# Decay gates moved into the input projection, the last down projection made a branch of the expert loop, and wide products beside the router

## The chip, the cores and the metric

The kernel runs on one core of a Trainium2 chip. The metric is the device time of one execution in microseconds (us). A core has a matrix engine (TensorE, PE, which reads its weights in a separate step, PEld), two elementwise engines (VectorE, DVE, and ScalarE, ACT), a third one (GpSimd, POOL) that here mostly issues gathers and scatters, and SyncE (SP), which issues the other transfers. Each has an instruction queue of its own and runs it in order; they wait for one another on semaphores.

## The reference

One encoder layer over 1024 tokens of width 1024, in float32:

```python
h = rms_norm(x)
q, k, v, r, gf, gb, glu = split(h @ w_in)          # gf, gb: 16 columns each
la_f = log_sigmoid(gf @ w2_f + b_f) / 16           # decay per token and key column
la_b = log_sigmoid(gb @ w2_b + b_b) / 16
a = rms_norm(gla(q,k,v,la_f) + flip(gla(flipped,la_b))) * silu(r)   # 4 heads, dk 64, dv 128
b = silu(layer_norm(depthwise_conv31(glu_a * sigmoid(glu_g))))
x = x + concat(a, b) @ w_out
x = x + cross_attention(rms_norm(x), rms_norm(mem))                 # 256 memory tokens, 4 heads
h = rms_norm(x)
gates = softmax(top4(h @ router_w + router_b))     # 32 experts
x = x + sum over the 4 experts of gate * (swiglu(h @ w_up + b_up) @ w_down + b_down)
y = rms_norm(x)
```

The decays `la` are summed up along the tokens inside windows of 128; scores and states use exponentials of differences of these sums, so the sums of a head pair must exist before any scores but those of the first level can be made.

## The kernel before

**Order of the stages.** The order of work is written out by hand for each engine, in one block an engine. PE's block runs: transposes of the normed x; input projection; LayerNorm sums of the convolution branch; memory projections mixed with the gated linear attention (GLA) of head pair 0; pair 1; output projection; queries, cross attention and its output projection; router; expert visits; last down projection. Times in the profile for these: projection from 36 to 275 us, GLA up to 527, output projection to 621, cross attention to 930, router to 971, expert visits from 1029 to 2578, last down projection from 2598.6, final norm from 2634.6.

**Input projection.** `w_in` comes in eleven chunks of 256 columns over a ring of buffers (SP's loop over `chunks`; a load waits for the matmul group named in `used`). ACT rounds each chunk to fp32r (`wiH`, line 670), DVE makes the rest (`wiL`, L1240, `w_in_lo`), and PE multiplies three products of high and low parts per 128 rows (L1946). Groups are numbered by `n` over eight PSUM banks: a group with n of 8 or more waits for the drain of group n-7. Groups 0 and 1 are the 32 gate columns; ACT copies them to `gT` (L699). Chunks 1 to 4 are the two GLU halves, drained by ACT to `u_pad` (L706) and by a sigmoid (L716), and DVE starts the 31-tap convolution (L1295, L1299, 124 steps) after `w_in_lo(4)`. Group 18 and the following are queries and keys, then values and `r`.

**Gates.** After the LayerNorm of the convolution branch, `gates(p)` (PE, L2032) multiplies `gT` by the second gate matrix for the head pair p, four matmuls into banks 0 to 3. ACT takes the absolute value from PSUM (L792), then Exp (L795) and Ln (L797) in place in `KQ`. DVE takes the minimum with 0 (L1345, into `EX`), subtracts (L1352), sums each window by a scan (L1356, into `Bf` and `Rb`, 16 scans), copies the window totals to `TTd` (L1362, L1363) and turns the second direction into suffix sums (L1365, L1367). For pair 0 this stands ahead of its scores; for pair 1, `gates(1)` comes after pair 0's keys are turned, the minima come before pair 0's states (L1429), and the rest after the multiplication of `r` by the norm's gain (L1459), before the exponents of pair 1 (L1383). `Bf` and `Rb` are shared by both pairs. Pair 0's scores use `exponents`, an exponential on ACT (L806), products on DVE (L1402, L1404) and small matmuls (L2057), level by level; `memory_chunk` (L1985) lies between them on PE and is drained by ACT (L663). PE waits at `gates(0)` for the end of LayerNorm.

**Router.** For each of eight token tiles PE turns the tile by eight transposes (L2255) and then multiplies the tile before by the router's weights, eight matmuls of 32 columns (L2245, 16 records). DVE makes top-4 and positions from it.

**Experts.** There are `last_` + 1 visits, here 32 (`last_` is a register read from memory, here 31). A visit's weights come in chunks of 1 MB (`load_chunk`), ACT rounds them (`split_hi`, L1014) and DVE makes the low part (`lo_by_vector`, L1740). Each engine has a loop `Fori(1, NVIS)` with NVIS = 53 and, inside, one `If(t <= last_)`; the passes with t above `last_` (21 of them) do nothing but count and test. What is left of the last visit, its second half of down-projection weights (chunks 15 to 18) and the matmuls, drains and scatter on them, stands after the loop. Then SP reloads the sums, ACT squares them (L1168), DVE scales them (L1901 to L1909), and SP stores them.

**Base rows.** Before the loop SP loads chunks 4 to 7 of visit 0, stores the residual rows to `acc_dram` tile by tile as they become ready (`s_bdr`), waits for all eight, and goes on with chunks 8 and 9.

Of the kernel before, what the change touches and what calls it, by code (L numbers as in the profile page):

```python
# [59 lines left out]
EARLY_BASE = 6  # L60
# [5 lines left out]
def build(nc, A):  # L66

    with ExitStack() as ctx:
# [77 lines left out]
        TTd = sb("TTd", [P, 2, 2, TT], F, 203.25)  # L146
# [92 lines left out]
        for n in ("m", "x", "y", "z"):  # L239
# [12 lines left out]
        s_z, s_zabs, s_zln, s_zmin, s_la, s_scan, s_tot, s_rb, s_dec = (  # L252
            sem(n) for n in ("gate_product", "gate_abs", "gate_softplus", "gate_min", "log_decay", "scanned",
# [57 lines left out]
        used = ([("in", n) for n in (2, 6, 10, 14, 18, 22, 26, 34, 42, 54, 62)]  # L311
# [85 lines left out]
        def _(sp):  # L397
# [10 lines left out]

            for i in range(4):
                sp.dma_start(xres[:, 2 * i:2 * i + 2, :], x_in[:, 2 * i:2 * i + 2, :]).then_inc(s_xld[i], 16)  # L410
            for g, (w, c0) in enumerate(chunks):
                if 2 <= g < N_IN + NR:
                    last = used[min(g, N_IN + 1) - 2]
                    sp.wait_ge(s_mm[last[0]], last[1])
                elif g >= NR:
                    sp.wait_ge(s_mm[used[g - NR][0]], used[g - NR][1])
                if g == g_out:
                    sp.wait_ge(s_ket, 8)
                if g == g_out + 1:
                    sp.wait_ge(s_op, 32)  # L420
                sp.dma_start(ring[:, slot_of[g]], w[:, c0:c0 + 256].rearrange("(k p) n -> p k n", p=P)
                             ).then_inc(s_ring[slot_of[g]], 16)
                if g == 1:
# [40 lines left out]
            for t in range(TT):  # L464
                sp.wait_ge(s_bdr, 2 * (t + 1))
                sp.dma_start(acc_dram[P * t:P * (t + 1), :], xres[:, t, :]).then_inc(s_acc, 16)
            sp.wait_ge(s_acc, 16 * TT)
            for c in range(8, 4 + NRAW):
                load_chunk(0, c, e0, None, fresh=True)
            for c in range(4 + NRAW, 12):  # L470
# [3 lines left out]
            with sp.Fori(1, NVIS) as t:  # L474
# [6 lines left out]
            e_last = expert(last_)  # L481
            for c in range(15, 19):
                load_chunk(last_, c, None, e_last, last=True)
# [13 lines left out]
        def _(pool):  # L497
# [105 lines left out]
            with pool.Fori(1, NVIS) as t:  # L603
# [5 lines left out]
            scatter(last_)  # L609
# [3 lines left out]
        def _(act):  # L613
# [81 lines left out]
            for th in range(2):  # L695
# [5 lines left out]
                next_split()  # L701
            for c2 in range(2):
# [17 lines left out]
            for dst, sc in ((qT, GDK ** -0.5), (kT, 1.0)):  # L720
                for ft in range(2):
                    for th in range(2):
                        d = drain("in", n)
                        if n == 18:
                            act.wait_ge(norms["x"]["scaled"], TT)
# [26 lines left out]
            for c in range(CT):  # L752
                act.wait_ge(s_lnv, 2 * (c + 1))
                if c == 0:
                    act.wait_ge(s_mm["in"], 62)
# [30 lines left out]
            def softplus(p):  # L786
                if p:
                    act.wait_ge(s_gram, 16)
                for n in range(4):
                    d, th = n // 2, n % 2  # L790
                    act.wait_ge(s_z, 4 * p + n + 1)
                    nc.scalar.activation(KQ[:, d, 512 * th:512 * (th + 1)], PS[:, n, :], ACT.Abs,  # L792
                                         bias=PV[:, ZB + 2 * d + p:ZB + 2 * d + p + 1]).then_inc(s_zabs, 1)
                act.wait_ge(s_zabs, 4 * (p + 1))
                nc.scalar.activation(KQ[:], KQ[:], ACT.Exp, scale=-1.0).then_inc(s_zln, 1)  # L795
                act.wait_ge(s_zln, 2 * p + 1)
                nc.scalar.activation(KQ[:], KQ[:], ACT.Ln, bias=1.0).then_inc(s_zln, 1)  # L797

            def window_decays(p):
                act.wait_ge(s_tot, 2 * (p + 1))  # L800
                nc.scalar.activation(TTd[:, 1], TTd[:, 0], ACT.Exp, scale=1.0 / TAU).then_inc(s_dec, 1)
# [51 lines left out]
            softplus(0)  # L853
# [20 lines left out]
            softplus(1)  # L874
# [259 lines left out]
            with act.Fori(1, NVIS) as t:  # L1134
# [16 lines left out]
            both_last = has_tail(last_)  # L1151
            split_hi(last_, 15)
            for c in range(16, 19):
                wait_lo(act, last_, c - NSPL)
                split_hi(last_, c, first=True)
            drain_rows(last_ + 1, 0, both_last, c0=1)
# [1290 lines left out]
```

## Time and profile before

| | us |
|---|---|
| median of 3 runs | 2657.73 (2645.79 to 2658.1) |
| the profiled execution | 2655.09 |
| its span | 2653.3 |
| PE busy | 2399.1 (90%) |
| DVE busy | 1814.8 (68%) |
| ACT busy | 1286.2 (48%) |
| POOL busy | 366.5 (14%) |
| DMA | 523.03 MB, mean 197 GB/s |

A row of a timeline gives the start from the span's beginning, the length, engine, line, operation, tensors and shapes, the number of instructions in the row, and in brackets the idle time before it with what ended it; "issue" there is a wait for nothing that the profile shows. PE's matmuls are pipelined, so a row's length is a little more than the spacing of its instructions. PEclk is the granted clock of PE as a share of the full one. An fp32 matmul shows as two records, an fp32r one as one.

### The profile page before, as it was taken

How to read it: one execution, taken by the hardware profiler on the slowest of the kernel's cores; microseconds unless marked ns; L12 is line 12 of the kernel's file. 1: busy time of each engine (PE TensorE's matmuls, PEld its weight loads, DVE VectorE, ACT ScalarE, POOL GpSimd, SP SyncE). 2: the span in 40 equal slices, each digit the busy share in tenths (PEclk: the TensorE clock that was granted, in tenths of full speed). 3: DMA queues.
4: the chain of work that ended last, by engine and by line, in shares of the span. 5: the costliest groups of instructions: out<-in, count | busy, mean ns of one | idle time of the engine just before them, and what ended most of it. 6: DMA issues, size and time to landing. Idle time of an engine off the chain costs nothing.

```text
span 2653.3 us, 38454 instructions
## 1 busy us (share of the span) xinstructions
PE 2399.1 (90%) x13540; PEld 1952.5 (74%) x13605; DVE 1814.8 (68%) x1880; ACT 1286.2 (48%) x1418; POOL 366.5 (14%) x305
## 2 busy tenths in 40 slices
PE   6999785698978977899999999999999999999983
PEld 5889574497846975777777777787787777777762
DVE  4499588614043157788977787778777778988763
ACT  4212455403132124656755565566555556766543
POOL 0000000010000042122211211122122112222210
PEclk9999896698999959899999999999999999999996
DMA  3111210311100028989987897789787789999764
GB/s 137 48 48 49 80 34 17 124 45 32 48 16 1 11 103 295 322 305 321 367 292 252 262 317 252 232 280 327 258 279 244 240 296 315 345 363 311 251 220 147
DMA packets 263104, 523.03 MB, mean 197 GB/s; under 512 B 10812, under 2 KB 44912, under 8 KB 262928
## 3 DMA queue, kind: packets, MB, share of 16 engines
q1 hardware_dynamic: 246112, 466.30, 49.8%
q0 software_dynamic: 15008, 52.70, 8.5%
q10 hardware_dynamic: 1904, 2.90, 0.4%
q8 instruction: 59, 0.97, 0.1%
q14 instruction: 21, 0.17, 0.0%
HBM read 482.27 MB, written 39.58 MB: 197 GB/s over the span
## 4 chain that ended last, share of the span: by engine, by line
PE 76%; DVE 12%; issue 5%; ACT 5%; DMA 1%; DVEq 1%; ACTq 0%; POOL 0%; POOLq 0%
PE PS L2347 12%; PE PS L2349 11%; PE PS L2348 11%; PE PS L1946 9%; PE PS L2355 7%; PE PS L2352 6%; PE PS L2166 4%; PE PS L2232 3%; DVE wlo L1740 2%; PE PS L2317 1%; PE PS L2219 1%; ACT whi L1014 1%; PE PS L2184 1%; PE PS L2186 1%; PE PS L2185 1%
## 5 line engine op out<-in xcount | busy, mean ns | idle before, releaser
L1740 DVE TENSOR_TENSOR wlo<-raw,whi 128x2048 fp32r<-128x2048 f32 x387 | 878.9, 2287 | 208.9 <-ACT whi L1014 179.9
L1014 ACT CAST whi<-raw 128x2048 fp32r<-128x2048 f32 x387 | 731.1, 1911 | 189.6 <-PE PS L2355 137.3
L2347 PE MATMUL PS<-whi,xhi 128*128 128x512 f32 x1024 | 426.2, 416 | 33.4 <-DVE yb L1823 17.5
L2349 PE MATMUL PS<-whi,xlo 128*128 128x512 f32 x1024 | 402.3, 393 | 0.0
L2348 PE MATMUL PS<-wlo,xhi 128*128 128x512 f32 x1024 | 400.4, 391 | 0.0
L2349 PEld LDWEIGHTS PS<-whi,xlo 128*128 128x128 f32 x1024 | 193.2, 189 | 42.6
L2348 PEld LDWEIGHTS PS<-wlo,xhi 128*128 128x128 f32 x1024 | 193.8, 189 | 39.0
L2347 PEld LDWEIGHTS PS<-whi,xhi 128*128 128x128 f32 x1024 | 194.8, 190 | 37.6 <-DVE wlo L1740 3.3
L2347 PE MATMUL PS<-whi,hhi 128*128 128x512 f32 x512 | 203.2, 397 | 21.1 <-DVE wlo L1740 21.1
L2349 PE MATMUL PS<-whi,hlo 128*128 128x512 f32 x512 | 200.0, 391 | 0.0
L2348 PE MATMUL PS<-wlo,hhi 128*128 128x512 f32 x512 | 199.9, 390 | 0.0
L2355 PE MATMUL PS<-wlo,xtl 128*128 128x512 f32 x480 | 193.5, 403 | 0.0
L2352 PE MATMUL PS<-whi,xtl 128*128 128x512 f32 x480 | 187.5, 391 | 0.0
L562 POOL COPY idxc<-TG 128x2 uint32 (+1 forms) x34 | 22.1, 651 | 926.9 <-PE PS L2317 497.0
L1299 DVE SCALAR_TENSOR_TENSOR yT<-u_pad,CWT,yT 128x1024 f32<-128x1024 f32 x120 | 144.2, 1274 | 0.0
L1070 ACT ACTIVATE yb<-PS,row_gate 128x512 f32<-128x512 f32 x64 | 44.0, 688 | 200.1 <-PE PS L2355 137.4
L584 POOL DMA_INDIRECT acc_scratch<-yb,idxs x66 | 134.0, 2031 | 22.0 <-issue 22.0
L569 POOL DMA_INDIRECT xs<-h_scratch,idxc x68 | 132.8, 1953 | 20.2 <-issue 16.6
L1511 DVE TENSOR_TENSOR xres<-xres,PS 128x256 f32<-128x256 f32 x64 | 26.9, 421 | 149.3 <-PE PS L2166 75.7
L2347 PEld LDWEIGHTS PS<-whi,hhi 128*128 128x128 f32 x512 | 96.4, 188 | 41.3 <-DVE wlo L1740 21.3
L2355 PEld LDWEIGHTS PS<-wlo,xtl 128*128 128x128 f32 x480 | 90.0, 188 | 30.4 <-issue 13.6
L1056 ACT COPY low_up<-PS 64x512 f32<-64x512 f32 x60 | 35.0, 584 | 158.3 <-PE PS L2355 158.3
(395 smaller groups left out, 4560.8 us busy)
## 6 DMA issues: line engine op xcount, KB each, us to landing
raw<-in_exp_w_up SPq DMA_DIRECT2D x259, 1024.0 KB, 6.2
raw<-in_exp_w_down SPq DMA_DIRECT2D x128, 1024.0 KB, 6.8
ring<-in_w_in SPq DMA_DIRECT2D x11, 1024.0 KB, 5.3
xres<-in_x SPq DMA_DIRECT2D x4, 1024.0 KB, 10.0
ring<-in_xattn_wk SPq DMA_DIRECT2D x4, 1024.0 KB, 7.6
ring<-in_xattn_wv SPq DMA_DIRECT2D x4, 1024.0 KB, 5.0
ring<-in_w_out SPq DMA_DIRECT2D x4, 1024.0 KB, 7.0
xres<-in_x SPq DMA_DIRECT2D x1, 4096.0 KB, 18.8
```

The costliest lines, as they stand in the source:

```text
L569: nc.gpsimd.indirect_dma_start(xs[0:rows, b, :], None, h3_dram, bass.IndirectOffsetOnAxis(ap=idxc[0:rows, b:b + 1], axis=0)).then_inc(s_xs ...
L584: nc.gpsimd.indirect_dma_start(acc_dram, bass.IndirectOffsetOnAxis(ap=idxs[0:rows, b:b + 1], axis=0), yb[0:rows, b, :], None, compute_op=A ...
L1014: nc.scalar.copy(whi[:, chunk_slot(c, NSPL), :], raw[chunk_slot(c, NRAW)][:]).then_inc(s_whi, 1)
L1299: ins = nc.vector.scalar_tensor_tensor(out=yT[:, c, :], in0=uc, scalar=w, in1=yT[:, c, :], op0=ALU.mult, op1=ALU.add)
L1740: nc.vector.tensor_tensor(wlo[:, chunk_slot(c, NSPL), :], raw[chunk_slot(c, NRAW)][:], whi[:, chunk_slot(c, NSPL), :].bitcast(F), ALU.subtract
L1946: ins = pe.matmul(out, lhs, rhs, start=(k == 0 and i == 0), stop=(k == KT - 1 and i == 2))
L2166: ins = pe.matmul(bank_groups(n, 256), a, b, start=(k == 0 and i == 0), stop=(k == KT - 1 and i == 2))
L2347: pe.matmul(o, hi[:, k, :], wh, start=first and bias is None, stop=False)
L2348: pe.matmul(o, hi[:, k, :], wl, start=False, stop=False)
L2349: ins = pe.matmul(o, lo[:, k, :], wh, start=False, stop=stop and kk == 3)
L2352: pe.matmul(ot, both_parts, wh, start=first, stop=False)
L2355: ins = pe.matmul(ot, both_parts, wl, start=False, stop=stop and kk == 3)
```

## The change

- The gate products of both head pairs are made by PE directly after the two small transposes behind chunk 0, as groups 2 to 9 of the projection; PE waits first for both `gT` copies. The group numbers in `used`, `glu_tile` and the waits of later stages move up by 8.
- ACT copies the eight products to new buffers `Zg`, then makes absolute value, Exp and Ln of both pairs into new buffers `BR`. DVE makes minima, subtraction, scans, totals and suffix sums of pair 0 after `w_in_lo(2)`, and of pair 1 after `w_in_lo(3)`, in `Zg`, `BR` and one `TTd` for each pair.
- SP stores both `BR` (1 MB each) to memory behind the load of chunk 3, reloads pair 0's into `Bf` and `Rb` behind the last chunk of the projection, and pair 1's after pair 0's last use of them. `gates`, `gate_minima` and `cumulated` go from their old places; `memory_chunk(0)` goes ahead of the LayerNorm's sums of squares, and `scores(0, 0)` ahead of `memory_chunk(1)`.
- In the router PE makes a wide product (fp32r, 128 by 512, result unused, bank 7) after each four transposes and each four router matmuls: 32 in all.
- The loops run to NVIS + 1 and get an `Else` with an `If(t <= last_ + 1)` that holds what stood after the loop.
- `EARLY_BASE` 6 becomes 8; the base rows are stored in two halves, with chunks 8 and 9 loaded between.

```diff
-            for c in range(6):
-                if c == 1:
-                    pe.wait_ge(s_pvc, 2)
+            pe.wait_ge(s_dr["in"], 2)
+            for p in range(2):
+                for d in range(2):
+                    for th in range(2):
+                        if n == 6:
+                            pe.wait_ge(s_pvc, 2)
+                        if n >= 8:
+                            pe.wait_ge(s_dr["in"], n - 7)
+                        pe.matmul(bank_groups(n), W2[:, d, P * p:P * (p + 1)], gT[:, 512 * th:512 * (th + 1)],
+                                  start=True, stop=True).then_inc(s_mm["in"], 1)
+                        n += 1
+            for c in range(6):
                 chunk_T()
...
+            memory_chunk(0)
             pe.wait_ge(s_lna, CT)
...
-            gates(0)
-            memory_chunk(0)
+            scores(0, 0)
             memory_chunk(1)
-            scores(0, 0)
...
             pe.wait_ge(s_sel, 6)
-            gates(1)
             updates(0, 0, 14)
...
+            act.wait_ge(norms["x"]["scaled"], TT)
+            for p in range(2):
+                for d in range(2):
+                    for th in range(2):
+                        done = drain("in", n)
+                        nc.scalar.copy(Zg[p][:, d, 512 * th:512 * (th + 1)], bank_groups(n)).then_inc(done, 1)
+                        n += 1
+            def softplus(p):
+                act.wait_ge(s_pvc, 1)
+                act.wait_ge(s_dr["in"], 2 + 4 * (p + 1))
+                for d in range(2):
+                    nc.scalar.activation(BR[p][:, d, :], Zg[p][:, d, :], ACT.Abs, ...)
+                nc.scalar.activation(BR[p][:], BR[p][:], ACT.Exp, scale=-1.0)
+                nc.scalar.activation(BR[p][:], BR[p][:], ACT.Ln, bias=1.0)
+            softplus(0)
+            softplus(1)
...
-            for c in range(2, 4):
-                w_in_lo(c)
+            gate_minima(0)
+            w_in_lo(2)
+            cumulated(0)
+            gate_minima(1)
+            w_in_lo(3)
+            cumulated(1)
...
+            def reload_decays(p):
+                if p == 0:
+                    sp.wait_ge(s_spill, 2 * 16)
+                for i, to in enumerate((Bf, Rb)):
+                    sp.dma_start(to[:], br_dram[p, :, i, :]).then_inc(s_rel, 16)
...
+                if g == N_IN + 1:
+                    reload_decays(0)
                 if g == g_out:
+                    sp.wait_ge(s_ex, exps_of(0, "starts") + 2)
+                    reload_decays(1)
                     sp.wait_ge(s_ket, 8)
...
+                if g == 3:
+                    for p in range(2):
+                        sp.wait_ge(s_rb, 2 * p + 2)
+                        sp.dma_start(br_dram[p], BR[p][:]).then_inc(s_spill, 16)
...
+            def wide_product():
+                pe.matmul(PS[:, 7, :], oxL[:, KT - 1, 0:P], oxL[:, KT - 1, 0:512], start=True, stop=True)
...
-            with dve.Fori(1, NVIS) as t:
+            with dve.Fori(1, NVIS + 1) as t:
                 with dve.If(t <= last_):
...
-            both_last = has_tail(last_)
-            for c in range(15, 19):
-                lo_by_vector(last_, c)
-            tail_rows(last_ + 1, both_last, low=1)
+                with dve.Else():
+                    with dve.If(t <= last_ + 1):
+                        both_last = has_tail(last_)
+                        for c in range(15, 19):
+                            lo_by_vector(last_, c)
+                        tail_rows(last_ + 1, both_last, low=1)
```

## Rows read from the trace of the kernel before

**Rows 1.** The page: shares of the chain that ended last.

```profile
PE 76%; DVE 12%; issue 5%; ACT 5%; DMA 1%; DVEq 1%; ACTq 0%; POOL 0%; POOLq 0%
```

**Rows 2.** Chain of waits, 0 to 900 us: start, length, what.

```profile
50.45 176.69 PE PS L1946 x960
...
228.89 46.08 PE PS L1946 x384
```

**Rows 3.** Stretches: length; busy PE, PEld, DVE, ACT, POOL; PEclk, DMA share, GB/s.

```profile
50.00:100.00 50.00, 50.00 (x223) 41.40 (x223) 9.16 (x10) 11.62 (x15) 0.00 (x0) 1.00 0.21 64
299.50:301.00 1.50, 1.50 (x4) 0.77 (x5) 0.50 (x1) 0.97 (x1) 0.00 (x0) 1.00 0.00 0
302.00:304.00 2.00, 2.00 (x4) 0.66 (x2) 2.00 (x1) 0.00 (x0) 0.00 (x0) 0.50 0.00 0
516.00:519.50 3.50, 3.28 (x16) 2.88 (x14) 3.46 (x2) 1.94 (x4) 0.00 (x0) 0.50 1.12 346
519.80:522.00 2.20, 1.93 (x16) 1.73 (x16) 2.20 (x2) 1.34 (x4) 0.00 (x0) 1.00 1.15 383
930.00:975.00 45.00, 40.39 (x192) 40.28 (x192) 19.52 (x48) 11.81 (x19) 28.35 (x10) 0.50 0.32 115
```

**Rows 4.** PE timeline, 275 to 400 us: start, length, work [idle before <-releaser].

```profile
288.68 9.98 PE L2024 MATMUL PS<-o_gla,ones 128*128 128x512 f32 x16 [6.13 <-ACT o_gla L756]
299.44 5.42 PE L2032 MATMUL PS<-gT,W 32*128 32x512 f32 x8 [0.78 <-DVE sig L1313]
...
394.35 3.70 PE L2032 MATMUL PS<-gT,W 32*128 32x512 f32 x8
```

**Rows 5.** ACT timeline, 40 to 60 us.

```profile
51.21 1.04 ACT L699 COPY gT<-PS 32x512 f32<-32x512 f32 x2
```

**Rows 6.** DVE timeline, 60 to 275 us.

```profile
79.88 2.29 DVE L1240 TENSOR_TENSOR wiL<-ring,wiH 128x2048 fp32r<-128x2048 f32 x1 [20.39 <-ACT wiH L670]
...
236.50 35.96 DVE L1299 SCALAR_TENSOR_TENSOR yT<-u_pad,CWT,yT 128x1024 f32<-128x1024 f32 x30
```

**Rows 7.** DVE, then ACT, timeline, 310 to 346 us.

```profile
320.13 2.72 DVE L1345 TENSOR_SCALAR EX<-PS,PV 128x512 f32<-128x512 f32 x4
327.78 2.29 DVE L1352 TENSOR_TENSOR EX<-EX,KQ 128x2048 f32<-128x2048 f32 x1 [4.93 <-ACT KQ L797]
330.11 2.63 DVE L1356 TENSOR_TENSOR_SCAN Bf<-ones,EX 128x128 f32<-128x128 f32 x8
...
344.10 0.37 ACT L663 COPY kx<-PS 128x256 f32<-128x256 f32 x1 [3.08 <-PE PS L1985]
...
345.90 1.04 ACT L806 ACTIVATE EX<-EX 128x1024 f32<-128x1024 f32 x1
```

**Rows 8.** DVE timeline, 395 to 432 us.

```profile
396.39 3.24 DVE L1345 TENSOR_SCALAR EX<-PS,PV 128x512 f32<-128x512 f32 x4 [3.13 <-PE PS L2032]
...
410.42 4.42 DVE L1459 TENSOR_TENSOR r_tm<-r_tm,ngb 128x4096 f32<-128x4096 f32 x1
...
425.06 1.23 DVE L1383 TENSOR_TENSOR EX<-TTd,Bf 128x1024 f32<-128x1024 f32 x1
```

**Rows 9.** Chain of waits, 928 to 975 us.

```profile
934.68 3.25 PE PS L2245 x16
937.94 1.76 PE PS L2255 x8
```

**Rows 10.** PE, DVE, ACT timelines, 2590 to 2640 us.

```profile
2598.62 0.80 PE L2347 MATMUL PS<-whi,hhi 128*128 128x512 f32 x1 [21.14 <-DVE wlo L1740]
...
2596.28 8.90 DVE L1740 TENSOR_TENSOR wlo<-raw,whi 128x2048 fp32r<-128x2048 f32 x4 [12.93 <-issue]
...
2635.86 0.15 DVE L1909 TENSOR_SCALAR st<-st 128x1 f32<-128x1 f32 x1 [14.94 <-ACT sqs L1168]
...
2634.60 1.06 ACT L1168 ACTIVATE sqs<-xres 128x1024 f32<-128x1024 f32 x1 [12.94 <-DMA xres<-acc_scratch]
```

**Rows 11.** DVE's waits by releaser, 1080 to 2570 us: us, times, longest.

```profile
DVE wlo L1740 <- issue: 15.4, 18, 1.0
```


## What is predicted

> **What bounds the kernel now.** I read the page's chain shares first: TensorE (PE) stands for 76% of the chain that ended last, VectorE (DVE) for 12%, "issue" for 5% [rows 1]. A change that takes no matmul away can therefore win only where the chain leaves PE, and can lose wherever it adds to PE. The chain by pieces then shows the input projection as one unbroken PE piece of 176.69 us [rows 2]: whatever is put into it costs its full time. The stretches by engine show two more things: in 50 to 100 us DVE is busy 9.16 and ScalarE (ACT) 11.62 of 50 us while PE is busy all 50 at a granted clock of 1.00 (2.4 GHz; 0.50 is 1.2); and the router stretch runs at 0.50 throughout, PE busy 40.39 of 45 us [rows 3]. The timelines of single engines give the three places where PE waits for the gates or for loop passes: the first pair [rows 7], the second [rows 8] and the last down projection [rows 10].
>
> **Gates in the projection: what they cost.** Eight gate matmuls (32 rows, 512 columns, fp32) are put on PE between chunk 0 and chunk 1. Four of them show as 8 records, so eight are 16. Eight records took 3.70 us at the later place and 5.42 at the earlier one [rows 4]; over that earlier one the clock was 1.00 in the first window and 0.50 in the next [rows 3]. Sixteen are thus 7.4 us at full clock. If the clock falls under them as it did there, after about six records, ten go at half (double 0.46, so 0.9 each): 2.8 + 9.0 = 11.8, and some of chunk 1's matmuls follow at half, for which I take 1.6. PE must also now wait for both copies of the low-rank gate rows, which ACT began at 51.21 and needed 1.04 us for [rows 5]; PE is there at 50.4, where chunk 1 now begins [rows 2], so 2 us are lost. Sum 15; at least 2 + 7.4 = 9.5, at most 17. I take 15, because the row at the first place fell in just this way.
>
> **What hides the rest of it.** ACT gets 8 copies of 0.6, 4 Abs of 1.0, 2 Exp and 2 Ln of 1.9 and their table loads (1.28 each), some 22 us; DVE gets four minima (under 1 us in all), and twice a subtraction (2.29), 16 scans (2.63 for eight), 0.3 and two of 1.2, some 24 us (DVE's and ACT's durations from rows 7; a copy or an Abs of 1024 columns is taken from the copies of rows 5). Both lie in the 50 us in which these engines were four fifths idle [rows 3]; in DVE's line one idle piece alone, before the split at 79.88, is 20.39 [rows 6]. The convolution then starts about when PE's delay starts it anyway, 15 us later. Its cover at the other end is thin: its last piece began at 236.50 and lasted 35.96 [rows 6], so ended at 272.5, and PE ended the projection at 275.0 [rows 2]. If DVE were delayed by its whole 24 us instead of 15, 6 us would show. I take 0, upper end 9 (none of the slack used), lower end 0. On SyncE's queue the two stores of decays stand behind the fourth load and ahead of the fifth, which has to wait for chunk 2 anyway; they wait for DVE's second cumulation, at about 107 where that load may go at about 109: 0 to 2, taken 0. The reloads come long before they are needed: 0. Putting a megabyte of memory traffic four times beside loads that use 0.21 of the queues there [rows 3] is in the same 0.
>
> **First pair.** Before, minima, softplus, subtraction, 16 scans and the suffix stood on the chain's way, from 320.13 to 330.11 + 2 x 2.6 + 0.3 + 2 x 1.2 = 338 [rows 7]. They go. What is late next is ACT's draining of the memory chunks: its last copies come every 3.45 us, the last at 344.10, and the exps only after it at 345.90 [rows 7]. These drains follow PE's memory matmuls, which no longer wait for the minima. One memory chunk (6.9 us) moves into PE's 6.13 us of idle ahead of the variance sums, which is 0.8 late; in return the sums' 16 records, 9.98 us now [rows 4], run at full clock in about 16 x 0.46 = 7.4. With that, LayerNorm ends 2 us earlier, ACT turns to the drains at about 317, and the four halves of chunks 2 and 3 take 4 x 3.45 and some 2 more for a first one at half clock: 333. With the table load and window decay (1.8 from the last copy to the exps, [rows 7]) the exps stand at about 335, not 345.9: **-10.9** in all. The bounds: -17 (all of the gating gone, drains no limit) and -5 (the drains follow nearly as before).
>
> **Second pair.** Minima for pair 1 (396.39, 3.24 us) go ahead of the state updates, and after them the run from the end of the gate's multiplication (410.42 + 4.42 = 414.8) to the exponents at 425.06 [rows 8], which is 10.3 us with PE idle. PE's own four gates (3.70, [rows 4]) go as well. The states start 2.8 us earlier, the exponents 2.8 + 10.3 = **13.1** earlier. PE's clock falls in that idle anyway, so no more is won; if the shorter idle kept it up, some 10 us more would come. Range -19 to -10.
>
> **Router.** Per token tile 8 transposes (1.76) and 8 matmuls (16 records, 3.25), 5.0 us, all at 0.50 [rows 9, 3]. 32 wide products are added, 4 per tile. In the projection 223 records of 512 columns fill 50 us at full clock, 0.224 each [rows 3]; at half 0.45. If the clock stays at half: 32 x 0.43 = +13.7. If it rises early: (5.0 / 2 + 4 x 0.23) x 8 = 27, plus about 4 at half before it rises, 31.5 against 40.4: **-9**. I take -9: elsewhere the clock went from 0.50 to 1.00 behind 3.5 us of transposes alone (516.0 to 519.5, then 519.8 [rows 3]), and here transposes and wide products together are over half of a tile's work. Range -11 to +13.7.
>
> The Trainium skill (TensorE: Matmul & The Clock Gate, Part 4: PE-mode transpose) says that transposes do not count as work for the clock as matmuls do. By that the eight transposes per tile would pull down what the four fillers lift. The row speaks against it: only transposes ran in 516.0 to 519.5, and the clock was 1.00 at 519.8 [rows 3]. By the rule the time would be that of rival B, by the row that of the forecast.
>
> **Base rows in halves, two more early loads.** Two loads move some 25 us earlier, the second half of the stores behind them. The gather at the head of the expert stage waits for none of it: 0 (-1 to +1).
>
> **Last down projection as a branch.** There are 21 passes of the loop with nothing to do. DVE's idle before its last four splits is 12.93 us of "issue" [rows 10], so 0.62 a pass, or up to 0.72 if its queue starts them under the split before; I use 0.68. PE waited 21.14 for that split. With the branch the split follows at once and PE waits 21.14 - 12.93 = 8.2: -12.9, less 1 as my allowance for code that has not run before: -12. But the 21 passes now stand between the last down projection and the final stage, with a second test in each. Let E be PE's end, 2618.5 (80 records from 2598.62 on). DVE's last drain ended at 2635.86 - 14.94 = E + 2.4 and it was needed again at E + 17.3; ACT at E + 16.1 [rows 10]. The passes begin when that drain is queued, about E + 1.6: DVE is free at E + 1.6 + 21 x 0.68 = E + 16 if a pass costs as before, at E + 24 if the second test adds half; ACT comes out alike. I take 6 us late, so **-6**; ends -12 and -2. In the live visits a jump over the other branch is added, hidden on ACT and DVE, whose queues run ahead: +1 (0 to +4, 31 visits by about 0.1).
>
> **Sum** against the profiled run's 2655.09 (span 2653.3 and 1.8 around it): +15 - 10.9 - 13.1 - 9 - 6 + 1 = -23, so 2632. Against the median 2657.73 it is 2634.7. The forecast is **2633**.
>
> **Rivals.**
> A better one: the gates run at full clock as at their later place (4 won, [rows 4]) and the tail's passes are hidden after all (6 won): 2632 - 4 - 6 = 2622. Against: both need the low end of their terms. Chance 0.12.
> B, the fillers do not lift the clock: +13.7 in place of -9, so 2632 + 22.7 = 2655, no change. For: the router stretch is already 90% busy and at 0.50 [rows 3], so busyness did not lift it; 32-column matmuls remain. Against: the fillers are wide. Chance 0.13.
> C, the convolution becomes the bound: ACT or DVE is not free when PE brings chunk 1, up to the whole 24 us show: 2632 + 24 = 2656. For: only 2.5 us of cover [rows 2, 6]. Chance 0.05.
> F, the skipped passes eat the tail's whole gain: 2638. Chance 0.06.
> E, slower: the longer loop body with a second branch makes each live visit pay a jump to code that isn't there. It decides from some 0.75 us a visit on, where 31 visits cost the 23 won. DVE's waits for issue are now 15.4 us in 18 times, the longest 1.0 [rows 11]; at 1.5 a visit it is 31 x 1.5 = +47, so 2632 + 47 = 2679. Against: a live visit takes the first test as before and jumps only at its end. Chance 0.06.
> My forecast keeps 0.58, own range 2620 to 2645.
>
> The Trainium skill (Runtime: NRT & Kernel Launch, Instruction fetch mechanics) says that a taken branch out of the fetched pages stalls until they come. It is the mechanism of E; its page gives no price, and no row here shows one beyond those counted.
>
> **Numbers.** What a measurement can tell from no change is about 0.5%, 13.3 us, so 2644.4 and 2671 are the marks. Faster: forecast 0.57 of its 0.58, A 0.12, F 0.04: 0.73. Slower: E and a bad sum of C and B: 0.07. Same: 0.20. Range 2612 to 2655.
>
> **What would show it.** Right: exps of the first pair about 38 us after the variance sums and not 47; pair 1's exponents about 13 us earlier against the state updates, and PE's idle there some 10 us shorter; clock near 1.00 in most of the router and its stretch about 32 us; PE's wait at the last down projection 8 us; DVE's first step of the final stage held by issue, not by ACT. Wrong: router clock 0.50 (B), DVE's convolution ending behind PE's projection (C), an issue gap at each visit (E), gates at 7.4 us (A).

## The result and the profile after

The changed kernel is slower, and it has become unsteady. Sixteen runs took 2648.5 to 2805.23 us, median 2676.73; sixteen of the kernel before took 2644.96 to 2658.1, median 2648.81. The ratio to before is 1.0051, 95% interval 1.0029 to 1.0073; the ratios here and below leave out runs in a slow state, which here is a kernel's own longest runs (five of these sixteen, six of the ten of e5), so the plain lists are given too. The forecast was 2633, with the time inside 2612 to 2655 and 0.07 on slower. The profiled run took 2706.32 us with a span of 2704.2, which is one of the longer ones.

I read the stages first, by the times at which PE begins each. In the changed kernel the input projection ends 14.7 us later than before (289.6 against 274.9), the output projection begins 16.6 earlier (510.5 against 527.1), the first token transposes 23.4 earlier (1003.5 against 1026.9). Up to there the change gains more than the 18 of the forecast's terms. From the first token transposes to the last visit's end it takes 1634.9 us, against 1550.6 before: +84 in 31 visits. From PE's end to the end of the span it is 37.1 against 34.8.

PE's waits in the visits, by releaser (us in total, times, longest); before, no wait for issue stood in this list:

```profile
PE PS L2410 <- issue: 67.5, 15, 7.0
PE PS L2410 <- DVE yb L1855: 7.7, 6, 1.5
```

The chain of waits at the end of one visit (start, length, what): the last transposes of the visit, 5.52 us of nothing that the profile shows, and the first product of the next visit:

```profile
1186.51 0.87 PE PS L2356 x8
1187.38 0.64 PE PS L2360 x8
1188.02 5.52 issue
1193.55 0.61 PE PS L2410
```

Section 3 of the page has a queue that reads instructions (packets, MB, share). First the kernel before, then the changed one, then the changed one from 1110 to 2560 us alone; in that last stretch the kernel before has no such row at all:

```profile
q8 instruction: 59, 0.97, 0.1%
```

```profile
q8 instruction: 89, 1.46, 0.2%
```

```profile
q8 instruction: 29, 0.48, 0.1%
```

A packet is 0.97 / 59 = 16.4 KB. PE's program of the kernel before has 15,256 instructions by my count of the built program, which is 59.6 blocks of 256 instructions, and 59 packets came: no block was fetched twice. In the changed kernel 29 are fetched again during the visits, two a visit, in the visits up to 1858 us and none after. The second of the two always falls in the wait: the jump that closes the If body was under way from 1186.24 for 5.98 us, a block was fetched at 1189.85, and the closing jumps of 15 visits took 3.9 to 7.6 us each. In both profiles that have such visits the refetching ends with one packet more, 3.1 us after the last pair (at 1858.0 here, at 1619.6 in e5). The clock is 1.00 before the wait and 0.50 behind it (columns as in [rows 3]):

```profile
1180.00:1186.00 6.00, 6.00 (x28) 4.99 (x27) 6.00 (x5) 2.78 (x3) 2.21 (x1) 1.00 0.74 245
1193.50:1196.00 2.50, 2.45 (x6) 2.04 (x7) 1.56 (x2) 0.00 (x0) 0.00 (x0) 0.50 1.06 213
```

The other places, in the order of the prediction. What follows the gates on PE (chain, 0 to 1100 us), and the gates' own row with the wait ahead of it [rows 2, 4]:

```profile
63.47 178.31 PE PS L1980 x960
...
243.53 46.08 PE PS L1980 x384
```

```profile
51.12 12.35 PE L2037 MATMUL PS<-gT,W 32*128 32x512 f32 x16 [1.85 <-ACT gT L725]
```

Pair 0's exponentials on ACT [rows 7] and pair 1's exponents on DVE (L1417) [rows 8]:

```profile
347.96 0.37 ACT L689 COPY kx<-PS 128x256 f32<-128x256 f32 x1 [3.08 <-PE PS L2019]
...
349.77 1.99 ACT L840 ACTIVATE EX<-EX 128x1024 f32<-128x1024 f32 x2
```

```profile
400.06 10.33 DVE L1463 SCALAR_TENSOR_TENSOR ST<-ST,TTd,PS 64x128 f32<-64x128 f32 x28 [2.51 <-PE PS L2119]
410.42 4.42 DVE L1491 TENSOR_TENSOR r_tm<-r_tm,ngb 128x4096 f32<-128x4096 f32 x1
414.77 1.22 DVE L1417 TENSOR_TENSOR EX<-TTd,Bf 128x1024 f32<-128x1024 f32 x1
```

Stretches of the changed kernel: pair 1's, and the router's [rows 3]. Below them the same stretch of pair 1 before:

```profile
422.00:492.00 70.00, 45.76 (x1044) 36.28 (x1044) 53.31 (x81) 40.52 (x124) 0.00 (x0) 0.74 0.05 17
911.00:949.50 38.50, 35.87 (x224) 32.80 (x224) 23.92 (x40) 11.59 (x18) 27.40 (x9) 0.80 0.35 127
```

```profile
432.00:510.00 78.00, 54.09 (x1044) 43.71 (x1044) 53.77 (x83) 42.08 (x128) 0.00 (x0) 0.63 0.06 18
```

DVE's scaling of the router's tiles, one instruction each but for the first row:

```profile
909.85 3.68 DVE L1640 SCALAR_TENSOR_TENSOR h<-xres,st,gfb 128x1024 f32<-128x1024 f32 x3
...
919.20 5.11 DVE L1640 SCALAR_TENSOR_TENSOR h<-xres,st,gfb 128x1024 f32<-128x1024 f32 x1
...
924.85 4.46 DVE L1640 SCALAR_TENSOR_TENSOR h<-xres,st,gfb 128x1024 f32<-128x1024 f32 x1
```

The last down projection and the final stage on PE, DVE and ACT [rows 10]:

```profile
2647.17 0.80 PE L2386 MATMUL PS<-whi,hhi 128*128 128x512 f32 x1 [8.74 <-DVE wlo L1772]
```

```profile
2644.82 8.90 DVE L1772 TENSOR_TENSOR wlo<-raw,whi 128x2048 fp32r<-128x2048 f32 x4 [0.53 <-issue]
...
2689.09 0.21 DVE L1943 TENSOR_SCALAR st<-st 128x1 f32<-128x1 f32 x2 [19.57 <-ACT sqs L1202]
```

```profile
2684.90 1.28 ACT L1197 ACT_TABLE_LOAD   x1 [16.16 <-issue]
```

### The profile page after: what moved, and what is told of

Its sections match the earlier page's. It is cut to its first block, busy times and chain, and to the rows that moved or that the text cites. A ratio compares the mean times of both kernels' runs of the same rounds, so it can differ in the third digit from the quotient of the medians.

```text
span 2704.2 us, 38946 instructions
## 1 busy us (share of the span) xinstructions
PE 2412.1 (89%) x13636; PEld 1955.4 (72%) x13637; DVE 1822.1 (67%) x1876; ACT 1292.3 (48%) x1421; POOL 356.5 (13%) x305
## 4 chain that ended last, share of the span: by engine, by line
PE 80%; DVE 9%; issue 5%; ACT 4%; DMA 1%; DVEq 1%; ACTq 0%; POOLq 0%; POOL 0%; SPq 0%
PE PS L2386 13%; PE PS L2388 12%; PE PS L2387 12%; PE PS L1980 9%; PE PS L2394 7%; PE PS L2391 6%; PE PS L2198 3%; PE PS L2264 3%; PE PS L2356 2%; PE PS L2410 1%; PE PS L2251 1%; PE PS L2216 1%; PE PS L2217 1%; PE PS L2218 1%; PE PS L2019 1%
## 5 line engine op out<-in xcount | busy, mean ns | idle before, releaser
L2386 PE MATMUL PS<-whi,xhi 128*128 128x512 f32 x1024 | 435.6, 425 | 0.0
L2388 PE MATMUL PS<-whi,xlo 128*128 128x512 f32 x1024 | 409.0, 399 | 0.0
L2387 PE MATMUL PS<-wlo,xhi 128*128 128x512 f32 x1024 | 408.0, 398 | 0.0
L2386 PEld LDWEIGHTS PS<-whi,xhi 128*128 128x128 f32 x1024 | 200.3, 196 | 37.3 <-DVE wlo L1772 1.8
L2410 PE MATMUL PS<-bup,SEL 128*128 128x512 bf16 x128 | 53.2, 415 | 87.0 <-issue 76.4
L593 POOL DMA_INDIRECT xs<-h_scratch,idxc x68 | 121.4, 1785 | 20.8 <-issue 18.0
```

The costliest lines, as they stand in the source:

```text
L593: nc.gpsimd.indirect_dma_start(xs[0:rows, b, :], None, h3_dram, bass.IndirectOffsetOnAxis(ap=idxc[0:rows, b:b + 1], axis=0)).then_inc(s_xs ...
L2386: pe.matmul(o, hi[:, k, :], wh, start=first and bias is None, stop=False)
L2387: pe.matmul(o, hi[:, k, :], wl, start=False, stop=False)
L2388: ins = pe.matmul(o, lo[:, k, :], wh, start=False, stop=stop and kk == 3)
```

## The experiments

The times, in us. Kernels between two lines ran on one chip and share the runs of the kernel before.

| | what it is | median (lowest to highest, runs) | ratio to before, 95% |
|---|---|---|---|
| e1 | changed, loops as before | 2640.0 (2628.1 to 2646.9, 10) | 0.9947 (0.9926 to 0.9969) |
| e2 | changed, PE's loop as before | 2639.0 (2633.0 to 2639.9, 8) | 0.9937 (0.9920 to 0.9955) |
| e3 | before, PE's loop as changed | 2648.7 (2645.6 to 2655.5, 10) | 0.9995 (0.9979 to 1.0011) |
| e4 | changed, loops end at last_ + 1 | 2621.6 (2619.5 to 2626.4, 4) | 0.9892 (0.9861 to 0.9924) |
| | | | |
| e5 | changed, PE's loop at place 72 | 2693.4 (2640.0 to 2804.2, 10) | 1.0005 (0.9965 to 1.0045) |
| e6 | changed, PE's loop at place 0 | 2639.7 (2628.0 to 2642.3, 6) | 0.9941 (0.9917 to 0.9965) |
| e7 | changed, PE's loop at place 100 | 2633.0 (2631.0 to 2635.0, 4) | 0.9922 (0.9896 to 0.9948) |
| e8 | e4 without wide products | 2629.0 (2621.2 to 2634.7, 4) | 0.9907 (0.9873 to 0.9942) |
| | | | |
| e9 | e4, code ahead of visit 0 laid | 2626.7 (2618.1 to 2634.7, 4) | 0.9917 (0.9894 to 0.9941) |
| e10 | e9, POOL later | 2641.3 (2636.7 to 2644.8, 6) | 0.9963 (0.9948 to 0.9978) |
| e11 | before, gates moved alone | 2643.6 (2638.9 to 2650.8, 10) | 0.9974 (0.9960 to 0.9989) |
| | | | |
| e12 | changed, PE's Else shorter | 2635.4 (2621.2 to 2637.4, 6) | 0.9926 (0.9901 to 0.9950) |

### e1 to e3: is it the branch, and whose

```diff
 e1, all five engines; e2, PE alone; e3, the reverse of it in the kernel before
-            with pe.Fori(1, NVIS + 1) as t:
+            with pe.Fori(1, NVIS) as t:
...
-                with pe.Else():
-                    with pe.If(t <= last_ + 1):
-                        down(last_ + 1, pe.snap(tail_last, min_val=0, max_val=1), c0=3, read=0)
+            down(last_ + 1, pe.snap(tail_last, min_val=0, max_val=1), c0=3, read=0)
```

> The changed kernel with the loops of all five engines and the last down projection as they were before; gates, fillers, early loads stay. Theory L (the branch in the loop makes PE refetch code in live visits: 16 waits for issue, 76.4 us in the profiled run): the expert stage goes back to about 1550 us from the first token transposes to the end of the loop (1635 in the changed kernel), no instruction fetch inside the visits, and the time is the kernel before less what the parts ahead of the loop won in the trace (first token transposes at 1003.7 against 1026.9), so about 2648 - 23 = 2625. Rival M (the visits suffer from something else in the change: other data placement, the early loads or the halves of the base rows): the visits stay as long as in the changed kernel, 2650 to 2700.

> The changed kernel with only PE's loop and last down projection as before; ACT, DVE, POOL and SP keep the branch. Theory L with PE alone as the engine that pays: visits as before (1550 us), PE walks its 21 empty passes before the last down projection (some 15 us, the other engines are ready earlier), the passes of ACT and DVE stand ahead of the final stage: about e1's time less 3 to plus 2, 2622 to 2627. Rival N (any engine's longer loop costs, ACT and DVE too): visits longer than 1560 us, over 2635.

> The kernel before with only PE's loop and last down projection changed to the branch. Theory L: this alone makes the visits 10 to 150 us longer, with one or two blocks of code fetched per visit and PE waiting for issue at the end of the loop; 2660 to 2800, and scattered from run to run. Rival O (it takes the branch together with code shifted by the gates and fillers, that is where the loop happens to lie): no fetch in the visits, the same time as before within 0.3%.

e1 and e2 take the unsteadiness away and come out alike, 0.5 and 0.6% faster than before: the visits suffered from PE's part of the branch and from nothing of the other four engines. The visits take 1552.0 and 1553.5 us again. Against their own runs of before they win 14 and 17 us. Both missed their expected times, 2625 and 2622 to 2627: in e1's profile the first token transposes begin at 1012.3, only 14.6 us earlier than before, so what is missing was lost ahead of the loop (more below). e2 also lies above the 2635 named for rival N, but its visits are as short as e1's, which is what N denied. e3 went against theory L: PE's branch alone costs nothing, and its trace has one packet for each block and no more:

```profile
q8 instruction: 59, 0.97, 0.2%
```

So the loop with the branch is good where the kernel before has it, and bad 64 instructions further on. Those 64 are the router's 32 wide products, two instructions each; the gate products only change their place and add none. The first form of my theory, that an Else part costs fetches, fell; its rival, the place, stood.

### e5, e6, e7: the place alone

```diff
+            pe.addr_align(256, offset=72, max_nops=0)        # e6: offset=0, e7: offset=100
             with pe.Fori(1, NVIS + 1) as t:
```

> The changed kernel with one line more: PE's loop is laid so that its first instruction stands at place 72 of a block of 256 instructions (the blocks are the 16 KB pieces that the trace shows being fetched). By the program's count the end of a live visit then lies at place 246 of its block and the end of the loop, behind the 274 instructions of the Else part, at place 8 of the block after the next. Theory J (a jump that lands two blocks ahead finds nothing there, one block ahead it does): fetches in the visits and waits for issue at their ends as in the changed kernel, 2645 to 2800, scattered. Rival Q (what counts is how many blocks the loop covers, or some other thing of the change): with 5 blocks covered here as in e7, no difference between the two.

> The same line with place 0: a live visit ends at place 173, the end of the loop lies at place 191 of the next block. Theory J: no fetch in the visits, the visits last 1550 us, PE waits 9 us ahead of the last down projection, and the final stage starts 2 us late: 2654 less 14.5 (e1) less 10 = 2630. Rival Q: fetches as in e5.

> The same line with place 100: a live visit ends at place 17, the end of the loop lies at place 35 of the next block. Theory J: as e6, 2630 within 5. Rival R (whatever lies early in a block is good or bad by itself): anything between e5 and e6.

The three kernels differ in one number. Instruction packets of e5 and of e6, and e5's wait for issue in the visits; e6 has no such row in the visits:

```profile
q8 instruction: 82, 1.34, 0.2%
```

```profile
q8 instruction: 60, 0.98, 0.2%
```

```profile
PE PS L2410 <- issue: 50.4, 11, 6.8
```

At 72 the runs scatter over 164 us as in the changed kernel, at 0 and 100 over 14 and 4. The median moves by 54 to 60 us. e6 had been expected at 2630 and e7 at 2630 within 5. Theory J holds: what counts is whether the jump over the Else part (274 instructions) crosses one block boundary or two.

### e12: the length of the jump

```diff
-                        down(last_ + 1, pe.snap(tail_last, min_val=0, max_val=1), c0=3, read=0)
+                        down(last_ + 1, ..., c0=3, read=0, with_tail=True)   # all_groups(True) alone
```

> The changed kernel with the Else part of PE's loop made shorter: the last down projection only in its form with tail rows (this input's last visit has them), without the test and the second form, 168 instructions instead of 272. Everything ahead of it, the loop's place too, is as in the changed kernel. Theory J: a jump of 168 instructions (under 256) cannot land two blocks ahead from anywhere: no fetch in the visits, 2630 to 2640 as e6 and e7. Rival T (an Else in the loop at this place is what costs, whatever its length): fetches and waits for issue as in the changed kernel, 2645 to 2800.

```profile
q8 instruction: 59, 0.97, 0.2%
```

With the Else part at 168 instructions and all ahead of it untouched, nothing is fetched twice and the median is 2635.4. An Else of this length at this place is harmless; rival T fell. That the same holds for every Else under 256 instructions at every place follows from theory J and was not tried. This is also what the change gives when its loop lies well: 2635, where the forecast was 2633.

### e4, e8, e9: a loop without empty passes, and the head of visit 0

```diff
-            with pe.Fori(1, NVIS + 1) as t:
-                with pe.If(t <= last_):
-                    (body)
-                with pe.Else(): ...
+            with pe.Fori(1, last_ + 1) as t:
+                (body)
+            down(last_ + 1, ...)          # so on all five engines
```

> The changed kernel with loops that end at last_ + 1 (a register) with no test inside and nothing skipped; the last down projection stands after the loop. Theory L: no Else block to jump over and no empty pass at either place: visits as before, PE waits about 8 us before the last down projection instead of 21, the final stage starts where the sums arrive: e1's time less 12 to 13, about 2612. Rival P (it is the longer loop code or jumps in general that PE stumbles over): here the loop is a little shorter than before, so no difference to L in the visits; if a loop that ends on a register costs as an If does, 1 us a visit more, 2645.

> The kernel of e4 (loops that end at last_ + 1) without the 32 wide products of the router. If the products are worth what the trace shows (router stretch 40.4 before, 32 to 38 with them), the time is 3 to 7 us above e4's 2621.6, and the router stretch is at clock 0.50 again. But the code behind the router lies 64 instructions earlier, as in the kernel before; by theory J the jump at the head of visit 0 (337 instructions) then lands one block ahead and not two, and the wait there is 4 us as before and not 11: the two together leave e4's time within 4 us. Rival: the products cost more than they bring, and it is 3 to 10 us faster than e4.

> The kernel of e4 (loops that end at last_ + 1) with PE's code ahead of visit 0 laid at place 0 of a block, so that the jump of 337 instructions at the head of visit 0 lands one block ahead. Theory J: PE's wait between the first token transposes and the first product falls from 11 us (e4, and the changed kernel) to 5, as in the kernel before: e4 less 6, about 2616. Rival S (that wait is for DVE or a weight's load that e4 brought no earlier): the wait stays and so does the time, 2622.

e4 is the best version, 1.1% faster than before and 18 us under e1, with which it shares its runs of before (12 to 13 under e1, and 2612, had been expected). PE waits 8.12 us for the last split, and ACT is held in the final stage by the reload and not by passes (PE, then ACT timeline):

```profile
2563.32 0.80 PE L2374 MATMUL PS<-whi,hhi 128*128 128x512 f32 x1 [8.12 <-DVE wlo L1763]
```

```profile
2598.87 1.06 ACT L1193 ACTIVATE sqs<-xres 128x1024 f32<-128x1024 f32 x1 [12.63 <-DMA xres<-acc_scratch]
```

Waits of PE for issue, 980 to 2550 us, in e4 and then in e9:

```profile
PE PS L2374 <- issue: 9.1, 1, 9.1
```

```profile
PE PS L2374 <- issue: 5.1, 1, 5.1
```

The two are not the same wait. e4's is at the head of visit 0. In e9 that head waits for VectorE alone, and the wait for issue stands at the end of visit 0, where e4 has none (PE timeline of e9):

```profile
1008.93 0.99 PE L2374 MATMUL PS<-whi,xhi 128*128 128x512 f32 x1 [3.01 <-DVE xlo L1774]
1048.17 0.90 PE L2374 MATMUL PS<-whi,xhi 128*128 128x512 f32 x1 [5.10 <-issue]
```

From the first token transposes to the first fp32r product it is 11.0 us in e4, 5.0 in e9 and 4.9 in e8. So that part of theory J holds as well: the jump at the head costs nothing that shows when it lands one block ahead. But laying the code anew moved the stall: from the first token transposes to visit 1's first product it is 46.0 us in e4 and 44.2 in e9, and over all visits, to the last transposes, 1548.6 and 1548.8. The gain of 6 us that I expected did not come (2626.7 and 2621.6 in different sets, which is no difference within their intervals).

e8 differs from e4 in the router: clock 0.50 and 40.4 us of PE, against 0.92 and 31.6. The kernels' times don't separate them (ratios 0.9907 and 0.9892, intervals overlapping), so the products' worth is read from the stretch alone (e8, then e4; length, busy PE, PEld, DVE, ACT, POOL, clock, DMA share, GB/s):

```profile
920.00:961.50 41.50, 40.39 (x192) 40.29 (x192) 14.59 (x40) 11.61 (x18) 28.19 (x9) 0.50 0.33 120
```

```profile
919.00:952.00 33.00, 31.61 (x224) 28.97 (x224) 18.84 (x39) 11.60 (x18) 27.80 (x9) 0.92 0.41 149
```

### e10 and e11: the terms of the router and of the gates

```diff
 e10
+            pool.wait_ge(norms["z"]["scaled"], TT)
             part(nc.gpsimd.memset(bup[:], 0.0))
 e11: the changed kernel with EARLY_BASE = 6, one loop over the base rows,
      no wide_product() and the loops as before
```

> The kernel of e9 with POOL's preparation of the biases held until DVE has scaled the last tile of the router. In the changed kernel DVE's scaling of a tile took 5.1 us beside POOL's subtraction where it takes 1.3 alone, and PE waited for it. If that is what keeps the wide products from their full worth: DVE's scalings 1.3 us each, router stretch about 30 us at clock 1.00 after its first 4 us, and 2 to 6 us less in all than e9, if POOL's later end doesn't hold PE's bias products. Rival: POOL's 27 us then end behind the router and PE waits for them, 0 to 10 us more than e9.

> The kernel before with the gates made in the projection and nothing else (no wide products, loops and base rows as before). The prediction's terms for this are +15, -10.9 and -13.1, together -9; in the trace of the changed kernel the output projection begins 16.5 us earlier, in e1's 8.5. I expect 5 to 17 us less than the kernel before, the likeliest -9, and no fetch in the visits. Rival: the convolution is late behind DVE's added 24 us and half of it is lost, -4 or less.

In e10 DVE's scaling takes 1.27 us, PE's stretch 31.5 with a clock of 0.92, as worked out. But PE then waits 18.67 us, and e10 is slower than e9 by 15 (DVE, stretch, PE):

```profile
922.53 1.27 DVE L1632 SCALAR_TENSOR_TENSOR h<-xres,st,gfb 128x1024 f32<-128x1024 f32 x1
```

```profile
914.50:946.00 31.50, 31.35 (x224) 28.97 (x224) 13.11 (x37) 11.60 (x18) 7.57 (x3) 0.92 0.43 155
```

```profile
964.63 0.24 PE L2294 MATMUL PS<-Mb,beforeb 128*128 128x32 bf16 x2 [18.67 <-DVE Mb L1658]
```

The wait is not for the biases, as the expectation's rival had it (and its 0 to 10 us were exceeded). It is for DVE's top-4 comparisons, which now run beside POOL's work in their turn (e10, then e9, where POOL is done by then):

```profile
952.36 10.84 DVE L1654 TENSOR_TENSOR OH<-iot,IXf 128x256 f32<-128x256 f32 x4
```

```profile
950.48 1.80 DVE L1653 TENSOR_TENSOR OH<-iot,IXf 128x256 f32<-128x256 f32 x4
```

So e10 shows twice that POOL's work stretches DVE's. The profiles show how: in the changed kernel the scaling that begins at 919.20, just behind the start of a POOL subtraction (919.15 to 923.22), ends at 924.31, and one that begins at 924.85 inside the next (923.30 to 928.23) ends at 929.32. A scaling that begins inside a POOL instruction ends 1.08 to 1.10 us after that instruction, whenever it began; so it is, but for one (1.25), in all the profiles. In the profiles e10 is 19.7 longer than e9. Of this 11.5 lie ahead of the visits; the visits are 7.4 longer, with five instruction packets more in all (65 against 60), which was not followed up. e11 is 0.26% faster than before (0.11 to 0.40), 7 us; it was given as -9.

## Why the prediction was wrong

**Where it failed.** The step "In the live visits a jump over the other branch is added, hidden on ACT and DVE, whose queues run ahead: +1 (0 to +4)". On ACT and DVE it was hidden: e2, where four engines keep the branch, is as fast as e1. On PE it was 67.5 us of waits in the profiled run's visits, and the other 17 fit the half clock behind each wait (0.50 in 1193.5 to 1196.0 above; the three products of the up projection were busy for 1252.6 us, before 1228.9). Over the runs it came to some 14 to 170 us above the 2635 of e12 (on another chip). The longest is 170 / 31 = 5.5 us for each of 31 visits, by my estimate, about what one such visit cost in the profile (84 / 15 = 5.6). I had named it as rival E, with 1.5 us a visit and 0.06. Two things were missing. I priced the jump from DVE's waits [rows 11], when PE is the engine on the chain. And I did not count instructions: the Else part's 272 are more than one fetched block, and the wide products move the loop by 64.

**Gates, +15.** Measured: chunk 1 begins 13.0 later (63.47 against 50.45 [rows 2]), the projection ends 14.7 later. The gates took 12.35 us after a wait of 1.85, where I had 11.8 and 2. The clock fell under them as at their earlier place (0.65 in 51 to 57 us, 0.50 in 57 to 64). The convolution held nothing up (DVE ended it 2 us ahead of PE).

**First pair, -10.9.** The exps begin at 349.77 against 345.90 [rows 7]; with the 14.7 on top of it, that is 10.8 won. The limit is the one named: ACT's last copy at 347.96, 3.45 us after the one before.

**Second pair, -13.1.** The exponents begin at 414.77 against 425.06 [rows 8]: a further 14.2. Behind them pair 1 ran at a clock of 0.74 in the changed kernel's profile against 0.63 before, which gave another 6. It doesn't always: in e1 the output projection begins only 8.5 us earlier, in e11's profile 13, and the same stretch of e1 has 0.65:

```profile
422.00:500.00 78.00, 52.20 (x1044) 41.60 (x1044) 54.66 (x82) 42.00 (x128) 0.00 (x0) 0.65 0.05 15
```

Of the gates together the runs say 7 us (e11), and I had 9.

**Router, -9.** The clock rose as forecast, but the stretch is 38.5 us and not 31.5, and e1 shows the same:

```profile
920.00:958.00 38.00, 36.04 (x224) 32.92 (x224) 23.07 (x37) 11.60 (x18) 27.41 (x9) 0.80 0.35 129
```

The term was mis-sized: -2 for -9. What failed is that DVE scales each tile beside POOL's subtraction and cast of the biases: 5.1, 4.5, 2.6, 2.7 and 1.9 us instead of 1.3. In the kernel before the same scalings took 1.6 to 1.9 us beside the same POOL work, because they happened to begin near the end of a POOL instruction, and a tile of 5.0 us at half clock hid that. At full clock PE comes back after 3.6 (e10), waits, and the clock falls in the wait. e10 shows the stretch without it, 31.5; e4's 33.0, with the same router code as the changed kernel's 38.5, shows how much the moments matter (its longest scaling took 4.17). The Trainium skill says that transposes don't count as the engine's work in the same way (TensorE: Matmul & The Clock Gate, Part 4: PE-mode transpose). As I had read it, that would have kept the clock at half here. It was at 0.80 to 0.92 with the wide products and at 0.50 without (e8, e11), which settles that the products together with transposes lift it, though not what transposes alone do there.

**Base rows, 0.** No wait on them in any trace. The code shift made the head of visit 0 longer by 7 us (11.0 against 4.0). Most of it comes back at the end of that visit, where the kernel before waits 4.80 us for issue and the changed one doesn't: to visit 1's first product it is 45.3 against 43.4.

**Tail, -6.** PE's wait went from 21.14 to 8.74, as worked out (8.2). The empty passes stand before the final stage and held ACT for 16.16 us, and DVE longer: its last pass ends at 2688.9, ACT had the first tile squared at 2687.4, and DVE's first step follows at 2689.09. Its row names ACT's square as the releaser, but the chain of waits there runs through DVE's passes. So DVE was held by its passes, as forecast. The second test made a pass 0.95 us on DVE and 0.82 on ACT, where one test took 0.68 and 0.59 before (spacing of the jumps), close to the half more that I had as the far case. DVE's first step comes at PE's end + 22.0 and not + 17.3. It is 4.7 late, but ACT had two tiles ready by then, and the end comes only 2.3 us late and not 6. So this term was -10.1.

**The sum without the failed step** is +14.7 - 10.8 - 14.2 - 2 - 10.1, about -22, where these terms were forecast at -24. That it comes so close is partly luck: the router is 7 short, the tail 4 and the second pair 1 beyond. e6, e7 and e12, which are the whole change with the loop in a harmless place, are 0.6 to 0.8% faster than before, 16 to 21 us. What they lack lies in pair 1's clock and in the visits (1562 us in e6, 1558 in e7). Of the 11 that e6's visits take more than before, 8 lie ahead of visit 1, where PE waits at the head and, 5.8 us, at the end of visit 0; the rest was not followed up.

**What is shown and what is not.** Shown: PE's branch, at this place, with this length, makes PE fetch two blocks a visit; moving the place or shortening the part ends it. The Trainium skill says that a taken branch to a page outside the fetched window stalls until it comes (Runtime: NRT & Kernel Launch, Instruction fetch mechanics). The trace agrees for a jump that lands two blocks ahead, with 3.9 to 7.6 us a jump. The same section of the Trainium skill gives this window as two pages, and for TensorE an instruction memory of 128 KiB, which is eight. Two is not what the runs show: in e7 the loop touches six blocks by the program's count, and its closing jump back over them fetched nothing from 1110 us on. Eight would hold the loop, but then it is open why one or two of its blocks are missing at all. Not shown: why a block stays missing through 15 visits and then stays in. It was 11 visits in e5's profile; each kernel has one profile, so that the number of such visits differs from run to run, and makes the scatter, is argued from the times alone. Nor was the loop's place in the changed kernel read from the chip: by the program's count it begins at place 25 after an unknown number of entry instructions, and theory J needs some 64 to 82.

## What to carry to other kernels

Before putting rarely run code into a loop on the engine that is the bound, count its instructions: if live iterations must jump over more than one fetch block (16 KB, 256 instructions here), it depends on the place whether they pay, and any edit ahead of the loop moves the place. Put such code after the loop, or keep it under a block, and end the loop on its real count if that is known at run time; then there are no empty passes to place at all (e4). When an edit removes a stall at one jump, look at the next jump before counting the gain (e9). And before moving GpSimd work out of the way, see what VectorE does where it goes (e10). A kernel whose runs scatter by several per cent after an edit to control flow should be looked at in the instruction queue's packets first.

## What the runs showed of the hardware

- A jump that lands two 16 KB blocks ahead can cost PE 3.9 to 7.6 us each time, beside weight loads at 275 GB/s (mean of the visits); one that lands one block ahead fetched nothing in the visits (e5 against e6 and e7).
- The refetching ended by itself, after 15 visits in the changed kernel's profile and 11 in e5's, each time with one packet more.
- A VectorE scaling of 1.27 us took up to 5.13 beside a GpSimd subtraction of 32 x 2048 elements: one that begins inside a GpSimd instruction ended 1.08 to 1.10 us after it, with one exception of 1.25. Four comparisons of 0.45 us each took 10.84 beside GpSimd's work (e10 against e9).
- Products whose result nobody reads lifted PE's clock in the router from 0.50 to between 0.80 and 0.92, and shortened its stretch by 2 to 8 us.
- An empty pass of a loop took 0.59 us on ACT, 0.68 on DVE and 0.73 on PE with one test, and 0.82, 0.95 and 1.09 with a second one inside (before against the changed kernel).
- A loop that ends on a register cost no more over the visits than one that ends on a constant with a test inside (1548.6 us in e4, 1550.6 before).
